# Up projection with the weights standing still and the activations moving, in a two-block transformer kernel on one core

## The reference

```
h = rms_norm(x, norm_mlp_pre)
u = square(relu(h @ w_up))            # 256 x 8192
x = x + rms_norm(u @ w_down, norm_mlp_post)
```

## Time and profile before

| | |
|---|---|
| median of 3 runs | 2007.04 us (2006.23 to 2007.12) |
| the profiled execution's own time | 2006.48 us |
| its span, first to last instruction | 2004.6 us |
| PE busy | 1986.4 us, 99% |
| PEld busy | 1650.4 us, 82% |
| DVE busy | 1171.2 us, 58% |
| ACT busy | 985.2 us, 49% |
| share of 16 DMA engines, weights' queue | 55.1% |
| mean granted clock of PE | 0.999 of full |

### The profile page before, as it was taken

The page is one execution under the profiler, slowest core; times in us unless marked ns, Lnnn a source line. Parts: engine busy times, 40 slices in busy tenths (PEclk is TensorE's granted clock), DMA queues, the critical chain, the costliest instruction groups (busy, mean ns, idle before and its releaser), DMA issues.

```text
span 2004.6 us, 22298 instructions
## 1 busy us (share of the span) xinstructions
PE 1986.4 (99%) x9216; PEld 1650.4 (82%) x9216; DVE 1171.2 (58%) x1081; ACT 985.2 (49%) x975; POOL 40.3 (2%) x42
## 2 busy tenths in 40 slices
PE   9999999999999999999999999999999999999998
PEld 7888888888888888888888888888898888887786
DVE  5746546645566644443356666677386858675555
ACT  6345544445445444444455555564556445454444
POOL 0000000000000000000000000000000000230000
PEclk9999999999999999999999999999999999999999
DMA  9554555455657366666555555574456444356443
GB/s 322 197 199 146 169 189 179 168 189 190 217 168 264 119 182 183 188 189 186 181 181 197 199 190 189 189 243 162 162 166 210 150 152 164 127 210 206 156 166 108
DMA packets 185437, 368.48 MB, mean 184 GB/s; under 512 B 6776, under 2 KB 14200, under 8 KB 184440
## 3 DMA queue, kind: packets, MB, share of 16 engines
q1 hardware_dynamic: 184472, 366.08, 55.1%
q10 hardware_dynamic: 864, 0.99, 0.1%
HBM read 364.94 MB, written 2.10 MB: 183 GB/s over the span
## 4 chain that ended last, share of the span: by engine, by line
PE 96%; issue 1%; DVE 1%; ACT 1%; DMA 0%; SPq 0%; POOLq 0%; POOL 0%; DVEq 0%
PE acc L1350 90%; PE mis L1350 4%; PE mis L1353 2%; ACT hi L486 1%; DMA raw<-in_w_in 0%; DVE m L860 0%; DVE lo L878 0%; SPq L342 0%; ACT ath L507 0%; DVE atl L908 0%; ACT spare L486 0%; DVE atl L882 0%; DVE xs L860 0%; ACT m L475 0%; DVE atl L915 0%
## 5 line engine op out<-in xcount | busy, mean ns | idle before, releaser
L878 DVE TENSOR_TENSOR lo<-raw,hi 128x2048 fp32r<-128x2048 f32 (+1 forms) x332 | 752.7, 2269 | 645.8 <-ACT hi L486 643.5
L1350 PE MATMUL acc<-hi,ath 128*128 128x512 f32 (+1 forms) x2672 | 1049.7, 393 | 5.7 <-DVE atl L908 1.6
L1350 PE MATMUL acc<-hi,atl 128*128 128x512 f32 (+1 forms) x2672 | 1034.7, 387 | 0.0
L1350 PE MATMUL acc<-lo,ath 128*128 128x512 f32 (+1 forms) x2672 | 1033.4, 387 | 0.0
L486 ACT ACTIVATE hi<-raw 128x2048 fp32r<-128x2048 f32 (+1 forms) x332 | 626.9, 1890 | 386.6 <-PE acc L1350 372.6
L1350 PEld LDWEIGHTS acc<-hi,ath 128*128 128x128 f32 x2672 | 501.9, 188 | 107.4 <-issue 4.2
L1350 PEld LDWEIGHTS acc<-hi,atl 128*128 128x128 f32 x2672 | 501.5, 188 | 102.2
L1350 PEld LDWEIGHTS acc<-lo,ath 128*128 128x128 f32 x2672 | 502.1, 188 | 98.1 <-issue 0.5
L475 ACT ACTIVATE m<-mis 128x512 f32<-128x512 f32 (+1 forms) x95 | 49.7, 523 | 217.0 <-PE mis L1353 188.0
L475 ACT ACTIVATE m<-acc,st 128x512 f32<-128x512 f32 (+2 forms) x104 | 69.8, 671 | 114.9 <-PE acc L1350 114.2
L860 DVE TENSOR_TENSOR m<-m 128x512 f32<-128x512 f32 (+2 forms) x119 | 72.3, 607 | 20.7 <-ACT m L475 15.7
(11 more groups left out here) (117 smaller groups left out, 553.8 us busy)
## 6 DMA issues: line engine op xcount, KB each, us to landing
raw<-in_w_in SPq DMA_DIRECT2D x134, 1024.0 KB, 5.1
raw<-in_w_up SPq DMA_DIRECT2D x64, 1024.0 KB, 5.5
raw<-in_w_down SPq DMA_DIRECT2D x64, 1024.0 KB, 5.0
raw<-in_w_out SPq DMA_DIRECT2D x32, 1024.0 KB, 5.1
raw<-in_w_pg SPq DMA_DIRECT2D x16, 1024.0 KB, 5.1
raw<-in_w_in SPq DMA_DIRECT2D x12, 688.0 KB, 4.2
raw<-in_w_a SPq DMA_DIRECT2D x8, 1024.0 KB, 5.1
raw<-in_w_b SPq DMA_DIRECT2D x8, 1024.0 KB, 5.0
```

The costliest lines, as they stand in the source:

```text
L878: e.tensor_tensor(lo, raw, hi.bitcast(F32), ALU.subtract).then_inc(s_lo.on("lo", n))
L1350: return e.matmul(o, a, b, start=start, stop=stop)
```

## The change

For blocks 1 to 15 of the up projection the roles are swapped. A 128 x 128 tile of the weights stands, and the activations move. ATH and ATL become halves of one tensor AT, so one matmul with the weights' high part moves 512 columns (256 tokens of the high part and 256 of the low part, two runs 16 tiles apart) and writes a whole PSUM bank: high x high to the left, low x high to the right. A second one with the weights' low part moves the 256 tokens of the high part alone and adds to the left half. Per channel tile there are 4 such pairs, one for each 128 of the block's 512 columns, each with a bank of its own; a block takes all four banks of `acc` (even blocks) or of `mis` (odd blocks). The sums come out with columns of w_up on the partitions, as UT needs them, so 30 of the 32 groups of transposes are gone; block 0 keeps its two, now in `acc`.

The two halves of a bank are summed after the block: ACT copies the right halves (128 x 1024) to UX, DVE adds the left ones, then DVE takes the maximum with 0 and multiplies by RB, and ACT squares into UT. RB is r1 laid out along the tokens on every partition, made once by two matmuls (`rb`) and an ACT copy. An even block now waits for the DVE addition two blocks back, block 1 for the last readers of `mis`, and block 2 for block 0's squares.

```diff
-            plan("up", j, w_up, 0, 16, 512 * j, 512, "r1")
+            plan("upw" if j else "up", j, w_up, 0, 16, 512 * j, 512, "r1")
@@ order of the side steps
-        for j in range(16):
-            for t in range(2):
-                beside(N_UP + 4 * j + 4 + t if j < 15 else N_DN - 1, "ut", j, t)
+        beside(N_UP + 4, "rb")
+        for t in range(2):
+            beside(N_UP + 5 + t, "ut", 0, t)
+        for j in range(1, 16):
+            beside(N_UP + 4 * j + 4, "ut", j, 1)
@@ ACT
+                if kind == "upw":
+                    ac.wait_ge(s_prod, "products", ids[-1], 1)
+                    act(UX[j % 2], column_banks(j)[:, :, S:2 * S], ACT.Copy).then_inc(s_act.on("low sums", j))
+                    return
@@ ACT, ut(j > 0)
+                    ac.wait_ge(s_dve, "up rows", j)
+                    act(UT[:, 4 * j:4 * j + 4, :], UX[j % 2], ACT.Square).then_inc(s_act.on("ut", j, 1))
@@ DVE, evac
+                if kind == "upw":
+                    z, u = column_banks(j), UX[j % 2]
+                    dv.wait_ge(s_act, "low sums", j)
+                    tt(u, z[:, :, 0:S], u, ALU.add).then_inc(s_dve.on("evac", b, 1))
+                    dv.wait_ge(s_act, "rb")
+                    stt(u, u, 0.0, RB.unsqueeze(1).broadcast_to([P, 4, S]), ALU.max, ALU.mult).then_inc(s_dve.on("up rows", j))
+                    return
@@ PE
+            def columns(n):
+                ...
+                pe.wait_ge(s_lo, "lo", n)
+                if k == 0:
+                    if block == 1:
+                        for i in range(4):
+                            pe.wait_ge(*held[i])
+                    elif block == 2:
+                        for t in range(2):
+                            pe.wait_ge(s_act, "ut", 0, t)
+                    else:
+                        pe.wait_ge(s_dve, "evac", b - 2, 1)
+                for j in range(4):
+                    for c in range(4):
+                        whole = (z[:, c, :], hv[:, j, c * P:(c + 1) * P], AT[:, :, k0 + j, :])
+                        half = (z[:, c, 0:S], lv[:, j, c * P:(c + 1) * P], ATH[:, k0 + j, :])
+                        if k + j == 0:
+                            mm(*whole, True, False)
+                            r = mm(*half, False, False)
+                        else:
+                            mm(*half, False, False)
+                            r = mm(*whole, False, k + j == nk - 1)
+                r.then_inc(s_prod.on("products", n, 1))
+                ...
+            def rb():
+                q = 2 * (number["wo", 3] % 2)
+                pe.wait_ge(s_pool, "r1")
+                pe.wait_ge(s_dve, "evac", number["wo", 3], 0)
+                for t in range(2):
+                    r = mm(acc[:, q, t * P:(t + 1) * P], ST[:, 52 + t:53 + t].broadcast_to([P, P]), IDN[:, :], True, True)
+                r.then_inc(s_pe.on("rb"))
```

More of the change, by code:

```diff
@@ L82, in program @@
         XS = sb("xs", [P, 2, D])
-        ATH = sb("ath", [P, 16, S], F32R)
-        ATL = sb("atl", [P, 16, S], F32R)
+        AT = sb("at", [P, 2, 16, S], F32R)
+        ATH, ATL = AT[:, 0, :, :], AT[:, 1, :, :]
         M = sb("m", [P, 80 * KB])
@@ L149, in program @@
         UT = m(0, 64 * S).rearrange("p (k s) -> p k s", k=64)
-        US = [t2(64, 512), t2(68, 512)]
+        US = t2(64, 512)
+        UX = [m(a, 1024).rearrange("p (c s) -> p c s", c=4) for a in (68, 72)]
+        RB = m(76, 256)
         VM, HV, GO = t2(0, 1024), t2(8, 1024), t2(16, 1024)
@@ L223, in program, with column_banks @@
         number = {(kind, j): b for b, (kind, j, n, ids) in enumerate(blocks)}
-        on_dve = ("rope", "a", "b", "wo", "z", "g", "res")
+        on_dve = ("rope", "upw", "a", "b", "wo", "z", "g", "res")
         def stage(name, g, t):
             return STG[name][(g if name in ("r1", "r2") else 2 * g + t) % 2]
+        def column_banks(j):
+            return mis if j % 2 else acc
         def freed(b):
@@ L586, in ut @@
             def ut(j, t):
-                ac.wait_ge(s_pe, "ut", j, t)
-                act(UT[:, 4 * j:4 * j + 4, t * P:(t + 1) * P], cut4(mis[:, place.get(("ut", j, t), 0), :]), ACT.Square).then_inc(
-                    s_act.on("ut", j, t))
+                if j == 0:
+                    ac.wait_ge(s_pe, "ut", 0, t)
+                    act(UT[:, 0:4, t * P:(t + 1) * P], cut4(acc[:, 2 * (number["wo", 3] % 2) + t, :]), ACT.Square).then_inc(
+                        s_act.on("ut", 0, t))
+                else:
+                    ac.wait_ge(s_dve, "up rows", j)
+                    act(UT[:, 4 * j:4 * j + 4, :], UX[j % 2], ACT.Square).then_inc(s_act.on("ut", j, 1))
+            def rb():
+                ac.wait_ge(s_pe, "rb")
+                act(RB, acc[:, 2 * (number["wo", 3] % 2), 0:S], ACT.Copy).then_inc(s_act.on("rb"))
             def prep(i):
@@ L708, in evac @@
                     if kind == "up":
-                        if j >= 2:
-                            ac.wait_ge(s_pe, "ut", j - 2, t)
                         ac.wait_ge(s_pool, "r1")
-                        act(US[j % 2][:, t, :], ps[t], ACT.Relu, scale=ST[:, 52 + t:53 + t]).then_inc(s_act.on("evac", b, t))
+                        act(US[:, t, :], ps[t], ACT.Relu, scale=ST[:, 52 + t:53 + t]).then_inc(s_act.on("evac", b, t))
                     if kind in ("nq", "hf", "qk", "hv", "vm", "go"):
@@ L778, in finish @@
                     e.dma_start(o_d[:, t, slice(*PIECES[1])], XS[:, t, slice(*PIECES[1])]).then_inc(s_out2.on("out", t), 16)
-            do = dict(lam=lam, da=da, na=na, sig=sig, ut=ut, cut=cut, prep=prep, conv=conv, gate=gate, hg=hg, ml=ml)
+            do = dict(lam=lam, da=da, na=na, sig=sig, ut=ut, rb=rb, cut=cut, prep=prep, conv=conv, gate=gate, hg=hg, ml=ml)
             def beside_products(n):
@@ L1411, in products @@
                 if k == 0 and b >= 2:
-                    pe.wait_ge(freed(b - 2), "evac", b - 2, t)
+                    pe.wait_ge(freed(b - 2), "evac", b - 2, 1 if blocks[b - 2][0] == "upw" else t)
                 for j in range(4):
@@ L1422, in products @@
                 r.then_inc(s_prod.on("products", n, t))
+            def columns(n):
+                src, w, b, k, nk, source, k0 = chunks[n]
+                block = blocks[b][1]
+                z = column_banks(block)
+                hv, lv = (y(n).rearrange("p (k c) -> p k c", c=w) for y in (hi_of, lo_of))
+                pe.wait_ge(s_lo, "lo", n)
[15 more added lines that the diff above has]
+                            r = mm(*half, False, False)
+                        else:
+                            mm(*half, False, False)
+                            r = mm(*whole, False, k + j == nk - 1)
+                r.then_inc(s_prod.on("products", n, 1))
+                if k + 4 == nk:
+                    for i in range(4):
+                        if block % 2:
+                            held[i] = (s_dve, "evac", b, 1)
@@ new lines, in rb, with ut @@
+            def rb():
+                q = 2 * (number["wo", 3] % 2)
[4 more added lines that the diff above has]
+                r.then_inc(s_pe.on("rb"))
+            def ut(j, t):
+                if j:
+                    return
+                z = acc[:, 2 * (number["wo", 3] % 2) + t, :]
+                pe.wait_ge(s_act, "rb")
+                pe.wait_ge(s_dve, "evac", number["wo", 3], t)
+                pe.wait_ge(s_act, "evac", number["up", 0], t)
+                for c in range(4):
+                    r = tr(z[:, c * P:(c + 1) * P], US[:, t, c * P:(c + 1) * P])
+                r.then_inc(s_pe.on("ut", 0, t))
@@ L1597, in turnover @@
                     products(c, 1)
-            do = dict(da=da, na=na, gate=gate, hg=hg, ml=ml)
+            do = dict(da=da, na=na, rb=rb, ut=ut, gate=gate, hg=hg, ml=ml)
             turn[0] = 0
@@ L1616, in tensor @@
                         unit(*u)
-                    products(n, t)
+                    if blocks[chunks[n][2]][0] != "upw":
+                        products(n, t)
+                    elif t == 1:
+                        columns(n)
                 for u in behind.get(n, ()):
```

3 lines of the change are left out of this document (removed).

## The result

| | before | after | forecast |
|---|---|---|---|
| median, us | 2007.14 (22 runs) | 2004.3 (22 runs) | 1998.6, range 1994.5 to 2003.0 |
| ratio | | 0.9987, 95% interval 0.9981 to 0.9993 | 0.9958 |
| profiled execution, us (span) | 2006.48 (2004.6) | 2003.52 (2001.6) | 1998.1 |
| PE busy | 1986.4 | 1984.1 | |
| DVE busy | 1171.2 | 1206.4 | |

The change gained 2.8 us, not 8.4. The page of the changed kernel answers to the earlier trace rows: PE still at 99% and full clock.

What follows compares the result with a forecast made beforehand. The prediction took PE's turns to bound the kernel. Its terms, -15.05 + 6.40 + 0.25 = -8.40 us, took the median from 2007.04 to 1998.6 us, with a range of 1994.5 to 2003 for 8 in 10.

Steps and rivals of the forecast that it cites:

- What bounds the kernel: Up projection: the chain of waits never leaves PE, so the stage's time is the sum of PE's turns.
- What goes, 15.05 us: PE's transpose groups of blocks 1 to 15 vanish: 13.58 us for blocks 1 to 14, 1.47 for block 15.
- What comes on PE, +6.40 us: Fixed charge of 8 more matmuls in each of 60 chunks, 106.7 ns a chunk, with loads hidden.
- `rb`, +0.25 us: Two float32 matmuls of 128 columns between PE's products add about 0.25 us; ends 0.22 and 0.47.
- Two runs, taken at nothing: The wide matmul's moving operand in two runs costs nothing extra; ends nothing or 12.8 us.
- ACT and DVE hidden, no added wait: Added ACT and DVE work at block ends stays hidden, with 5 us of cover, adding no PE wait.
- The sum: Whole kernel: -15.05 + 6.40 + 0.25 = -8.40 us, so a median of 1998.6 us.
- rival 1: Load not hidden behind the short matmul, at each wide one after it: +35.2 or +65.3 us; chance 0.06.
- Rival 2: Wide matmul's two runs cost a second start: +12.8 us, chance 0.06; a smaller part, 2000 to 2005, 0.04.
- slower: Outcome for the whole kernel: the change makes it slower; chance 0.12.
- within 0.2%: Outcome for the whole kernel: a change of at most 0.2% (4 us); chance 0.04.
- a wide one of 235 or more: Sign in PE's up projection: a wide turn of at least 235 ns would make the forecast wrong in sign.

Runs made afterwards that it cites:

- e5: The kernel before with PE's 30 groups of transposes of blocks 1 to 15 left out; 1991.85 us, ratio 0.9927.
- e4: The changed kernel with the short matmuls left out in blocks 1 to 15; 1882.99 us, less work done.
- e11: The changed kernel with the wide matmuls left out in blocks 1 to 15 except each block's first tile; 1881.9 us, less work done.
- e3: The changed kernel with AT laid out so that the wide matmul moves one run of 512 contiguous columns; 2004.45 us, ratio 0.999.
- e9: The order of e1 plus one transpose of the identity in block 2's first chunk, between a wide and a short matmul; 1999.51 us, ratio 0.9962.
- e1: The changed kernel with every pair issued wide first, then short, in every channel tile; 2004.98 us, ratio 0.9991.
- e10: The changed kernel with one added transpose of the identity in block 3's first chunk alone; 2003.87 us.
- e7: The changed kernel with one added transpose of the identity in the first chunk of each of blocks 2 to 15; 2000.95 us, ratio 0.9972.
- e2: The changed kernel with each tile's four short matmuls together, then four wide (first tile wide ones first); 2002.5 us, ratio 0.9978.

## Why the prediction was wrong, point by point

- **What bounds the kernel**: right. PE's turns, before and after.
- **What goes, 15.05 us**: right, 15.01 in e5's trace (15.04 by the medians).
- **What comes on PE, +6.40 us**: this step failed. "16 x 226.67 + 16 x 120.0 = 5546.7 ns" takes a turn's price from its width alone. Both prices are true for turns of one kind (e4, e11), and the sum is true in the even and double patterns, but 53 of the 60 chunks ran in the triple one at 5.65. The term was 6.40 and measured 11.95 (6.40 + 5.46 + 0.09). I had bounded the short turn by its neighbours' widths, and never asked whether a sequence of unequal turns has a price of its own; the kernel before had only runs of equal ones in its products.
- **`rb`, +0.25 us**: 0.46. The trace shows four records of 0.11 us for it, not two, and the chunk behind it took 6.008 us against 5.547. That is within the ends given, 0.22 and 0.47.
- **Two runs, taken at nothing**: right (e3, e4).
- **ACT and DVE hidden, no added wait**: right, to 0.1 us.
- **The sum**: -8.40 forecast, -2.63 measured in the stage; e9, which removes the slow pattern from block 2's first chunk on, is at 1999.51, 0.9 us from the forecast of 1998.6.
- **The rivals**: rival 1 named the place (a wide matmul behind a short one) and the shape (a few ns, 960 times) but only large sizes for it and 128.7 as the point where it decides; the pair came out 6.7 ns over the forecast's, under the 8.7 that would have used up the whole gain. Rival 2 had 0.04 for a small cost of that size, by a mechanism that e3 and e4 exclude. The range's upper end, 2003.0, was 1.3 us too low. By the rivals' own chances "slower" should have read 0.14 (0.06 + 0.06 + 0.02) and "within 0.2%" 0.02.
- **The signs**: "a wide one of 235 or more" was to mean a wrong sign. Wide turns did average 236 ns in blocks 3 to 15, yet the sign held, because the short turns beside them averaged 117. Even the fast even pattern has 230 and 117. Only the pair's sum could tell.

## What to carry to other kernels

Where TensorE bounds a stage and unequal matmuls alternate on it, price the sequence and not the turns: measure the distance over whole periods in several places of a stretch, and where the same instructions run at two paces, look at the joints ahead of them. Unbroken alternation over tiles and blocks keeps the pace it has, the slow one too (e1); it pays only together with something that sets the fast one, as e9's one inserted turn did. One inserted turn and another order of the first tile are both cheap to test. A forecast of this kind needs room for a charge of a few ns a turn, even where each kind's own price is exact.

## What the runs showed of the hardware that was not expected

- A steady stream of alternating 256- and 512-column fp32r matmuls showed three patterns: 230 / 117 ns (period one pair), a period of two pairs (0.693 us), both 346.7 ns a pair, and a period of three pairs (1.060 us), 353.3 a pair. The even one ran on for 880 pairs (e9) and the triple one through blocks 2 to 15 of e1, through waits that were already met and changes of bank; the double one was seen only inside a block, since each block's joint ended it.
- A single 128-column transpose followed by a short matmul led from the triple pattern to the even one both times it was tried (e10's block 3, e9's block 2), and from the double one to the even one in all 14 blocks of e7. In e1, where a wide matmul follows, a group led once to the even one (the chunk behind `rb`, 5.995 us) and twice to the triple (6.09).
- Shorts in a row took 120 ns, wides in a row 227, wides behind a run of shorts 234 falling to 229 over the run of four (e2).
- The fixed charge of 13.33 ns was there only at the full clock. In e11 PE waited 2.43 us for DVE, and then the granted clock was 0.50 for a while; PE in order of time, inside that stretch:

```profile
872.52 2.98 PE L1375 MATMUL mis<-at,lo 128*128 128x256 f32 x13
```

  Less the last record's 0.42, (2.98 - 0.42) / 12 = 213 ns a short turn: 256 columns at the 1.2 GHz level and nothing more, where the full clock gave 120.0, 13.3 above its 106.7.
- Why the patterns differ is not settled. The records show loads starting 2 to 5 ns behind the start of the matmul before in all of them, so no load is visibly late; whether it is the load path, the read of the moving operand or the issue was not separated by these runs.
